# Attention rows scaled on GpSimd, two attention stages ordered by feature tile, value products ahead of turns

## The chip, the cores and the metric

One core of one Trainium2 chip runs the whole kernel in one launch. The metric is the device time in microseconds (us); the time quoted is the median of several runs.

## The reference, cut to what matters

The program is four layers of a transformer on 512 tokens of 1024 features, all in float32. Two of its parts are touched here. Both are attention with 16 query heads and 4 key/value heads of 64 features.

```
# sparse attention (NSA), first layer: two branches, "selected" and "window"
p_s = softmax(where(dist_s >= 0, q k_s + bias_s, NEG));  o_s = p_s v_s
p_w = softmax(where(m_w,         q k_w + bias_w, NEG));  o_w = p_w v_w
o = gate0 * o_c + gate1 * o_s + gate2 * o_w
y = (o * silu(z)) @ w_out
# sliding window attention (SWA), last layer: window of 128 keys and a sink logit per head
p = exp(s - m) / (sum(exp(s - m)) + exp(sink - m));      y = (p v) @ w_o
```

With 512 tokens both NSA branches see every earlier key, so a 128-query tile i (0 to 3) has 128(i+1) keys in NSA, and 256 keys (128 for i = 0) in SWA. The compressed branch o_c is ready before the stage starts and lies in `oT`.

## The kernel before, in words

The kernel is a list of stages (`build`). Every engine runs its part of each stage in order and ends it in `end_stage` (L2894 to L2897), where it waits until TensorE, ScalarE, VectorE and GpSimd have all ended theirs. Large products use three passes: weights and activations are split into a high part (fp32r) and the rest, the low part. ScalarE makes the high part of a weight slot of 512 KB (`split_hi`, L259), GpSimd the low part (`split_lo`, L270); the rings hold three slots.

**NSA, stage `NsaAttend`.** A *pair* is one feature tile k of 128 features (two heads, `st` 0 and 1), one query tile i and one branch br: 64 pairs, in the order i = 3, 2, 1, 0, then k, then br. TensorE works in rounds. Round u issues S(u), T(u-2), V(u-3):
- S, scores (L1264): two products in the two halves of the array, into two of four PSUM banks.
- T, turns (L1275): 2(i+1) transposes of 128x128 of the exponentials, into banks 4 and 5.
- V, value products (L1288): 2(i+1) products into bank 6 + br.

VectorE adds the bias and takes the row minimum (L1368), ScalarE takes the exponential with the row sum (L1325). VectorE copies the turned head 0 out of PSUM (L1377), ScalarE head 1 (L1333). The row sums are divided out only later. After every 8 pairs (a *batch*: four k, two branches) VectorE makes the reciprocals times the gate (L1383, L1386), TensorE spreads these columns over the 64 features of each head with 16 small products (L1298), and VectorE copies the spread out of PSUM and multiplies with banks 6 and 7 (`combine`, L1393 and L1394). The next batch's first V waits for that (L1284), since it writes the same banks. GpSimd then adds the two branches into `oT` and multiplies by z (L1352, L1353, L1355).

**Output, after NSA.** Only when the stage has ended on all engines does ScalarE round `oT` to the high part (L785) and VectorE and GpSimd take the low part (L897, L836), tile k by tile k, and TensorE's projection (L358 high, L368 low, in `project_tokens`) waits for each.

**SWA, stage `SwaAttend`.** The same scheme: 32 pairs (i, k), i outermost, batches of 4. L1955 are its scores, L1966 turns, L1978 value products, L1989 the spread, L2056 the bias, L2021 the exponential, L2065 and L2029 the copies (VectorE two thirds of them, ScalarE every third pair). VectorE and ScalarE also work out the sink's term per batch (L2072, L2042, L2079, L2080), and `combine` is L2087 and L2088. The spread here takes a turn in the four score banks, so the next scores wait for `combine`. `SwaProject` comes before it and also splits the first two weight slots of the output projection; `NsaAttend` splits its two at its own start.

Of the kernel before, what the change touches and what calls it, by code (L numbers as in the profile page):

```python
# [7 lines left out]
ALU = mybir.AluOpType  # L8
# [6 lines left out]
P = 128  # L15
T = 512
# [427 lines left out]
class Stage:  # L444
    def __init__(self, env):
        self.env = env
# [258 lines left out]
class Output(Stage):  # L705
# [3 lines left out]
    def __init__(self, env, w_out, g_row, oT, o=None, z=None, kd=KD, following=None, whole=None):  # L709
        super().__init__(env)  # L710
        self.o, self.oT, self.kd, self.g_row, self.z, self.whole = o, oT, kd, g_row, z, whole
# [5 lines left out]
        if o is not None or whole is not None:  # L717
            env.ots += KD
# [35 lines left out]
    def turned(self, k):  # L754
        if self.whole is not None:
            return self.whole[:, k, :]
# [20 lines left out]
    def scalar(self, act, step):  # L777
        env, nc = self.env, self.env.nc
        env.split_hi(act, self.lds[0])
        for k in range(KD if self.o is not None or self.whole is not None else 0):  # L780
            if self.z is not None:
                act.wait_ge(env.otmp_ready, self.tmp0 + k + 1)
            elif self.o is not None:
# [44 lines left out]
    def gpsimd(self, pool, step):  # L828
# [3 lines left out]
        if self.z is not None or self.whole is not None:  # L832
# [16 lines left out]
    def vector(self, dve, step):  # L849
        env, nc = self.env, self.env.nc  # L850
        if self.whole is not None:
            for k in range(0, KD, 2):
                self.low(dve, k)
# [353 lines left out]
class PairAttend(Attend):  # L1207

    def __init__(self, env, prefix, pairs, per):
# [3 lines left out]
        self.scale_ready, self.spread_ready = env.sem(prefix + "scale_ready"), env.sem(prefix + "scale_spread")  # L1215

        self.uses = []
        for step in range(len(pairs) + 4):
            if step < len(pairs):
                self.uses.append(("scores", step))  # L1220
            if step >= per + 2 and (step - 2) % per == 0:
                self.uses.append(("spread", (step - 2) // per - 1))
        self.use = {key: n for n, key in enumerate(self.uses)}

    def banks(self, kind, n):
        at = 2 * (self.use[kind, n] % 2)
        return self.env.ps[:, at:at + 2, :]

    def wait_banks(self, pe, kind, n):

        at = self.use[kind, n] - 2
        if at >= 0:
            before, m = self.uses[at]
            if before == "scores":
                pe.wait_ge(self.s_biased, 2 * m + 2)
            else:
# [1783 lines left out]
```

## Time and profile before

| | |
|---|---|
| median of 3 runs | 2593.06 us (2592.02 to 2595.28) |
| the profiled execution's own time | 2606.13 us |
| its span, first to last instruction | 2604.3 us |
| TensorE matmuls busy | 2266.0 us (87%) |
| ScalarE, VectorE, GpSimd busy | 983.2, 926.0, 794.2 us |
| mean granted TensorE clock | 0.886 of full speed |

The span is one execution's; 1.8 us lie around it. Busy matmul time is modelled, so what TensorE's idle time and the rounds' lengths say counts for more than its busy share.

### The profile page before, as it was taken

To read this page: it belongs to the slowest core of one execution; us is meant where nothing else is said; L and a number is where in the kernel's file an instruction comes from. 1 tells how busy PE (TensorE), PEld (TensorE's weight loads), DVE (VectorE), ACT (ScalarE), POOL (GpSimd) and SP (SyncE) were. 2 spreads that over 40 slices of the span, in tenths; PEclk is the share of its full clock that TensorE was granted. 3 is DMA by queue.
4 is the path that set the end of the run, shared out by engine and by line. 5 is a ranking of instruction groups with operands and counts; after the bars stand their busy time and mean duration, and the time that the engine had idled before them with its cause. 6 is when DMAs were issued, how large, how long until landed. Compare 5 with 4: busy or idle time off the path is not lost.

```text
span 2604.3 us, 32281 instructions
## 1 busy us (share of the span) xinstructions
PE 2266.0 (87%) x12952; PEld 1782.8 (68%) x12954; DVE 926.0 (36%) x1861; ACT 983.2 (38%) x1841; POOL 794.2 (30%) x376
## 2 busy tenths in 40 slices
PE   5999788799987879984599969999897888999898
PEld 4898565578765647743488647888687656888787
DVE  1100455430028464257343354333104164333401
ACT  3331255442245353353134425444215344444412
POOL 2331011234420324324000143444442303444442
PEclk9987699699998879966569879999999989999999
DMA  4222000023220112201101022333322202333322
GB/s 121 74 69 76 22 1 1 9 81 92 89 73 1 61 49 77 83 4 25 31 7 27 28 81 65 97 93 96 107 94 73 66 1 65 89 97 94 94 96 81
DMA packets 222423, 162.16 MB, mean 62 GB/s; under 512 B 31451, under 2 KB 206115, under 8 KB 222275
## 3 DMA queue, kind: packets, MB, share of 16 engines
q1 hardware_dynamic: 219762, 151.91, 19.9%
q0 software_dynamic: 2512, 8.19, 1.0%
q8 instruction: 104, 1.70, 0.3%
q14 instruction: 45, 0.36, 0.0%
HBM read 154.83 MB, written 5.24 MB: 61 GB/s over the span
## 4 chain that ended last, share of the span: by engine, by line
PE 52%; DVE 8%; ACT 3%; issue 2%; DMA 1%; POOL 1%; POOLq 0%; DVEq 0%; SPq 0%; ACTq 0%; PEld 0%; PEldq 0%
PE ps L358 11%; PE ps L329 8%; PE ps L328 8%; PE ps L332 8%; PE ps L368 5%; PE ps L2581 2%; PE ps L2539 2%; PE ps L1955 1%; PE ps L1966 1%; PE ps L1978 1%; ACT buffer L2636 1%; DVE buffer L2207 1%; PE ps L2604 1%; PE ps L2551 1%; PE ps L2230 1%
## 5 line engine op out<-in xcount | busy, mean ns | idle before, releaser
L270 POOL TENSOR_TENSOR weights_lo<-buffer,weights_hi 128x1024 fp32r<-128x1024 f32 (+1 forms) x265 | 658.3, 2486 | 1017.7 <-ACT weights_hi L259 1017.3
L259 ACT ACTIVATE weights_hi<-buffer 128x1024 fp32r<-128x1024 f32 (+1 forms) x265 | 276.3, 1045 | 315.5 <-PE ps L368 306.6
L328 PE MATMUL ps<-u_hi,weights_hi 128*128 128x512 f32 (+1 forms) x752 | 281.5, 378 | 6.4 <-DVE u_lo L642 5.9
L329 PE MATMUL ps<-u_lo,weights_hi 128*128 128x512 f32 (+1 forms) x752 | 285.1, 383 | 0.0
L332 PE MATMUL ps<-u_hi,weights_lo 128*128 128x512 f32 (+1 forms) x752 | 176.9, 378 | 0.0
L1786 ACT ACTIVATE buffer<-ps,buffer 128x512 f32<-128x512 f32 x88 | 68.5, 779 | 282.6 <-PE ps L332 282.6
L1816 DVE SCALAR_TENSOR_TENSOR buffer<-ps,buffer,buffer 128x511 f32<-128x511 f32 x88 | 66.0, 750 | 292.0 <-ACT buffer L1786 292.0
L328 PEld LDWEIGHTS ps<-u_hi,weights_hi 128*128 128x128 f32 x752 | 143.5, 191 | 33.2 <-DVE u_lo L642 6.5
L2636 ACT ACTIVATE buffer<-ps 32x128 f32<-32x128 f32 (+4 forms) x240 | 92.6, 393 | 188.2 <-PE ps L2581 64.7
L329 PEld LDWEIGHTS ps<-u_lo,weights_hi 128*128 128x128 f32 x752 | 143.1, 190 | 29.3
L332 PEld LDWEIGHTS ps<-u_hi,weights_lo 128*128 128x128 f32 x752 | 136.8, 191 | 26.6 <-POOL weights_lo L270 0.2
L358 PE MATMUL ps<-weights_hi,act_hi 128*128 128x512 f32 x352 | 113.3, 404 | 17.7 <-DVEq L2897 17.7
L872 DVE RECIPROCAL buffer<-buffer 128x1 f32<-128x1 f32 x24 | 3.8, 160 | 347.6 <-ACT buffer L797 347.5
L358 PE MATMUL ps<-weights_hi,act_lo 128*128 128x512 f32 x352 | 112.6, 401 | 0.0
L1325 ACT ACTIVATE buffer<-buffer,buffer 128x512 f32<-128x512 f32 (+3 forms) x128 | 71.5, 558 | 91.2 <-DVE buffer L1368 91.1
L1368 DVE CUSTOM_DVE_ANT_0 buffer<-ps,buffer 128x512 f32<-128x512 f32 (+3 forms) x128 | 62.0, 486 | 88.9 <-PE ps L1264 88.9
L368 PE MATMUL ps<-weights_lo,act_hi 128*128 128x512 f32 x352 | 91.9, 395 | 0.0
L358 PEld LDWEIGHTS ps<-weights_hi,act_hi 128*128 128x128 f32 x352 | 67.8, 193 | 34.2 <-DVEq L2897 18.5
L328 PE MATMUL ps<-nsa_u_hi,weights_hi 128*128 128x512 f32 x192 | 78.7, 410 | 7.4 <-PEq L2897 5.7
L2853 POOL DMA_DIRECT2D buffer<-in_gn_g x1 | 0.6, 600 | 275.1 <-ACTq L2897 275.1
L328 PE MATMUL ps<-mix_hi,weights_hi 128*128 128x512 f32 (+2 forms) x160 | 67.9, 424 | 18.6 <-DVE mix_lo L2195 12.8
L328 PE MATMUL ps<-diff_u_hi,weights_hi 128*128 128x512 f32 (+1 forms) x216 | 78.8, 372 | 4.5 <-DVE diff_u_lo L642 3.4
(380 smaller groups left out, 4625.6 us busy)
## 6 DMA issues: line engine op xcount, KB each, us to landing
buffer<-in_w_up SPq DMA_DIRECT2D x88, 512.0 KB, 3.8
buffer<-in_w_down SPq DMA_DIRECT2D x44, 512.0 KB, 3.2
buffer<-in_diff_w_in SPq DMA_DIRECT2D x32, 512.0 KB, 4.0
buffer<-in_nsa_w_in SPq DMA_DIRECT2D x28, 512.0 KB, 3.8
buffer<-in_w_rkv SPq DMA_DIRECT2D x24, 512.0 KB, 3.8
buffer<-in_nsa_w_out SPq DMA_DIRECT2D x8, 512.0 KB, 3.6
buffer<-in_diff_w_out SPq DMA_DIRECT2D x8, 512.0 KB, 3.5
buffer<-in_norm_g POOLq DMA_DIRECT2D x8, 512.0 KB, 4.0
```

The costliest lines, as they stand in the source:

```text
L259: self.nc.scalar.activation(self.part_hi[:, part % self.PARTS, 0:n], self.raw[:, ld % self.RAW, 0:n], ACT.Copy).then_inc(self.hi_ready, 1)
L270: self.nc.gpsimd.tensor_tensor(self.part_lo[:, part % self.PARTS, 0:n], self.raw[:, ld % self.RAW, 0:n], self.part_hi[:, part % self.PARTS ...
L328: nc.tensor.matmul(out, hi[:, k, :], rhs[0][:, k, tokens], start=(k == 0), stop=False)
L329: nc.tensor.matmul(out, hi[:, k, :], rhs[1][:, k, tokens], start=False, stop=False)
L332: mm = nc.tensor.matmul(out, lo[:, k, :], rhs[0][:, k, tokens], start=False, stop=(k == KD - 1))
L358: nc.tensor.matmul(out(i, b), lhs[part][:, index * m + k, i * P:(i + 1) * P], hi[:, k, b * width:(b + 1) * width], start=(index + k == 0 a ...
L368: mm = nc.tensor.matmul(out(i, b), lhs[0][:, index * m + k, i * P:(i + 1) * P], lo[:, k, b * width:(b + 1) * width], start=False, stop=stop)
L1325: nc.scalar.activation(m.p[:, at, 0:n], m.p[:, at, 0:n], ACT.Exp, scale=-1.0, bias=m.nmax[:, at:at + 1], accum_out=m.psum[:, total:total + ...
L1368: nc.vector.tensor_tensor_reduce(m.p[:, at, 0:n], self.banks("scores", u)[:, st, 0:n], m.bias[:, 2 * k + st, T - n:T], -1.0, 1e38, ALU.add ...
L1786: nc.scalar.activation(m.conv[:, 2 * (j % 2) + half, :], env.bank(g), ACT.Identity, scale=self.col(2, half, j), bias=self.col(3, half, j)) ...
L1816: step(nc.vector.scalar_tensor_tensor(c[:, 1:T], env.bank(g)[:, 0:T - 1], self.col(1, half, j), c[:, 1:T], ALU.mult, ALU.add))
L2636: copy = lambda dst, src: nc.scalar.activation(dst, src, ACT.Copy)
```

## The change

- In both stages k becomes the outer loop. NSA's order is (k, i, br) with i = 3, 1, 2, 0; SWA's is (k, i) with i = 3, 2, 1, 0.
- Right after a pair's exponentials VectorE takes the reciprocals of its two row sums (`invert`), and GpSimd multiplies the exponentials by them in place, 128 rows by 128(i+1) columns per head, two instructions per pair; in NSA the gate is a second factor of the same instruction. The spread, `combine`, and the additions on GpSimd are gone.
- A tile k gathers in one PSUM bank, 6 + k % 2: in NSA both branches and all i, 512 columns. One VectorE addition per k takes it into `oT` (`take`); GpSimd multiplies by z and takes the low part, ScalarE the high part. For the last k VectorE does GpSimd's share.
- In SWA GpSimd writes the sink as one more column of the scores, and the exponential and its sum take it in. ScalarE and VectorE take the high and low part of each k straight from PSUM.
- The round is S(u), V(u-4), T(u-3) in place of S(u), T(u-2), V(u-3); the ring of exponentials has four slots in place of three.
- TensorE doesn't wait for the end of these two stages; the output projection waits for tile k's low part and for the banks. The output projection no longer makes the high and low parts.
- One more weight slot is split ahead in both places.

```diff
 class Output(Stage):
     def tensor(self, pe):
-        ready = (lambda k: self.wait_turned(pe, k)) if turns or self.whole is not None else None
+        ready = (lambda k: self.wait_turned(pe, k)) if turns else None
+        if self.before is not None:
+            self.before.wait_banks_free(pe)
+            ready = lambda k: self.before.wait_result(pe, k)
...
 class PairAttend(Attend):
+    AHEAD = 3
+    SLOTS = 4
+    def invert(self, dve, u):
+        at = self.slot(u, 0)
+        dve.wait_ge(self.p_ready, 2 * u + 2)
+        self.env.nc.vector.reciprocal(self.m.scale[:, at:at + 2], self.m.psum[:, at:at + 2]).then_inc(self.inverse_ready, 1)
...
 class NsaAttend(PairAttend):
-        super().__init__(env, "nsa_", [(i, k, br) for i in reversed(range(NT)) for k in range(KD) for br in range(2)], 8)
+        super().__init__(env, "nsa_", [(k, i, br) for k in range(KD) for i in (3, 1, 2, 0) for br in range(2)], 8)
...
     def tensor(self, pe):
         def scores(u):
-            self.wait_banks(pe, "scores", u)
+            if u >= 2:
+                pe.wait_ge(self.s_biased, 2 * (u - 2) + 2)
...
         def turn(u):
             for st in range(2):
-                pe.wait_ge(self.p_ready, 2 * u + st + 1)
+                pe.wait_ge(self.p_scaled, 2 * u + st + 1)
...
-        for step in range(n_pairs + 4):
+        for step in range(n_pairs + self.AHEAD + 1):
             if step < n_pairs:
                 scores(step)
-            if 2 <= step <= n_pairs + 1:
-                turn(step - 2)
-            if 3 <= step <= n_pairs + 2:
-                values(step - 3)
-            if step >= 10 and (step - 2) % 8 == 0:
-                spread((step - 2) // 8 - 1)
+            if step - self.AHEAD - 1 >= 0:
+                values(step - self.AHEAD - 1)
+            if 0 <= step - self.AHEAD < n_pairs:
+                turn(step - self.AHEAD)
...
     def gpsimd(self, pool, step):
+        def scale(u):
+            k, i, br = self.pairs[u]
+            n = P * (i + 1)
+            pool.wait_ge(self.inverse_ready, u + 1)
+            for st in range(2):
+                at, gate = self.slot(u, st), 3 * (2 * k + st) + 1 + br
+                p = m.p[:, at, 0:n]
+                nc.gpsimd.tensor_scalar(p, p, m.scale[:, at:at + 1], m.gate[:, i, gate:gate + 1], ALU.mult,
+                                        ALU.mult).then_inc(self.p_scaled, 1)
...
+        for u in range(n_pairs):
+            scale(u)
+            if u % self.per == 3 and u > self.per:
+                gated(u // self.per - 1)
+            if u % self.per == 7 and u > self.per:
+                low(u // self.per - 1)
...
     def vector(self, dve, step):
+        def take(k):
+            dve.wait_ge(self.pv_done, self.per * (k + 1))
+            o = m.oT[:, k, :]
+            nc.vector.tensor_tensor(o, env.ps[:, 6 + k % 2, :], o, ALU.add).then_inc(self.o_taken, 1)
...
+        for u in range(n_pairs + self.AHEAD):
             if u < n_pairs:
                 bias(u, 0)
+            if u >= self.AHEAD:
+                copy(u - self.AHEAD)
             if u < n_pairs:
                 bias(u, 1)
+            if 1 <= u <= n_pairs:
+                self.invert(dve, u - 1)
+            if u % self.per == 4 and u > self.per:
+                take(u // self.per - 1)
...
 class SwaProject(Stage):
-        self.env.split_lo(pool, self.q[-1][0] + 2)
+        self.env.split_lo(pool, self.q[-1][0] + 3)
...
 class SwaAttend(PairAttend):
-        super().__init__(env, "swa_", [(i, k) for i in reversed(range(NT)) for k in range(KD)], 4)
+        super().__init__(env, "swa_", [(k, i) for k in range(KD) for i in reversed(range(NT))], NT)
...
+        def high(k):
+            act.wait_ge(self.pv_done, self.per * (k + 1))
+            nc.scalar.activation(m.u[0][:, k, :], env.ps[:, 6 + k % 2, :], ACT.Copy).then_inc(self.hi_ready, 1)
...
+        def sink(u):
+            k, n, at = self.pairs[u][0], self.width(u), self.slot(u, 0)
+            if u >= self.SLOTS:
+                pool.wait_ge(self.pT_ready, u - self.SLOTS + 1)
+            nc.gpsimd.tensor_copy(m.p[:, at:at + 2, n], m.nsinks[:, 2 * k:2 * k + 2]).then_inc(self.sink_put, 1)
+        def scale(u):
+            pool.wait_ge(self.inverse_ready, u + 1)
+            for st in range(2):
+                at = self.slot(u, st)
+                p = m.p[:, at, 0:self.width(u)]
+                nc.gpsimd.tensor_scalar(p, p, m.scale[:, at:at + 1], None, ALU.mult).then_inc(self.p_scaled, 1)
...
+        def low(k):
+            dve.wait_ge(self.hi_ready, k + 1)
+            nc.vector.tensor_tensor(m.u[1][:, k, :], env.ps[:, 6 + k % 2, :], m.u[0][:, k, :].bitcast(F32),
+                                    ALU.subtract).then_inc(self.lo_ready, 1)
...
-def end_stage(env, eng, s):
+def end_stage(env, eng, s, goes_on=False):
     eng.drain().then_inc(env.stage_done, 1)
-    eng.wait_ge(env.stage_done, 4 * (s + 1))
+    if not goes_on:
+        eng.wait_ge(env.stage_done, 4 * (s + 1))
```

## Rows read from the trace of the kernel before

**Rows 1.** Windows (stretch, length, PE, PEld, DVE, ACT, POOL busy, clock, DMA) of both stages.
```profile
314.00:516.80 202.80, 171.59 (x1474) 112.45 (x1473) 108.77 (x353) 101.15 (x324) 34.20 (x28) 0.87 0.02 6
2071.90:2160.40 88.50, 72.94 (x593) 47.70 (x593) 54.18 (x191) 43.26 (x151) 1.00 (x2) 0.83 0.02 7
```

**Rows 2.** Timeline around the first batch border of NSA: start us, us, engine, line.
```profile
346.73 1.09 PE L1275 MATMUL ps<-buffer,buffer 128*128 128x128 f32 x8
...
349.91 1.23 DVE L1394 TENSOR_TENSOR buffer<-ps,buffer 128x1024 f32<-128x1024 f32 x1
...
351.28 1.98 PE L1288 MATMUL ps<-buffer,buffer 128*64 128x128 f32 x16 [3.46 <-DVE buffer L1394]
```

**Rows 3.** Windows of 5 us in NSA; the third number from the end is the clock.
```profile
341.00:346.00 5.00, 5.00 (x62) 3.87 (x63) 2.06 (x6) 2.65 (x7) 0.00 (x0) 1.00 0.01 2
...
351.00:356.00 5.00, 4.72 (x24) 2.92 (x25) 0.83 (x3) 0.00 (x0) 3.80 (x3) 0.50 0.00 0
476.00:481.00 5.00, 5.00 (x28) 2.68 (x24) 1.69 (x12) 2.83 (x14) 1.55 (x2) 0.50 0.02 5
```

**Rows 4.** Timeline, end of NSA and start of its output projection.
```profile
505.04 1.22 PE L1288 MATMUL ps<-buffer,buffer 128*64 128x128 f32 x8
...
516.80 1.19 PE L358 MATMUL ps<-weights_hi,nsa_u_hi 128*128 128x512 f32 x2 [8.36 <-DVE nsa_u_lo L897]
...
518.81 3.93 DVE L897 TENSOR_TENSOR nsa_u_lo<-buffer,nsa_u_hi 128x512 fp32r<-128x512 f32 x2 [0.57 <-ACT nsa_u_hi L785]
```

**Rows 5.** Timeline, the start of weight slots 1 and 3 (counted from 0) of that projection.
```profile
524.20 0.62 PE L358 MATMUL ps<-weights_hi,nsa_u_hi 128*128 128x512 f32 x2
...
535.27 0.62 PE L358 MATMUL ps<-weights_hi,nsa_u_hi 128*128 128x512 f32 x2
```

**Rows 6.** Timeline, TensorE's scores and turns of an i = 2 round, and the next scores.
```profile
388.28 0.92 PE L1264 MATMUL ps<-buffer,buffer 64*128 64x384 f32 x4
389.12 0.87 PE L1275 MATMUL ps<-buffer,buffer 128*128 128x128 f32 x6
...
390.73 0.59 PE L1264 MATMUL ps<-buffer,buffer 64*128 64x384 f32 x2
```

**Rows 7.** Timeline, SWA's last pairs (128 keys) at full clock: scores, turns, value products.
```profile
2152.21 0.50 PE L1955 MATMUL ps<-buffer,buffer 64*128 64x128 f32 x4
...
2152.64 0.44 PE L1966 MATMUL ps<-buffer,buffer 128*128 128x128 f32 x2
...
2153.00 0.44 PE L1978 MATMUL ps<-buffer,buffer 128*64 128x128 f32 x4
```

**Rows 8.** Groups by line and shape in NSA (busy us, mean ns of one).
```profile
L1325 ACT ACTIVATE buffer<-buffer,buffer 128x512 f32<-128x512 f32 x32 | 23.0, 719 | 23.9 <-DVE buffer L1368 23.9
L1368 DVE CUSTOM_DVE_ANT_0 buffer<-ps,buffer 128x512 f32<-128x512 f32 x32 | 21.7, 686 | 28.7 <-PE ps L1264 28.7
L1333 ACT ACTIVATE buffer<-ps 128x512 f32<-128x512 f32 x16 | 9.2, 578 | 0.3 <-PE ps L1275 0.3
```

**Rows 9.** GpSimd's groups by line and shape, whole span.
```profile
L270 POOL TENSOR_TENSOR weights_lo<-buffer,weights_hi 128x1024 fp32r<-128x1024 f32 x261 | 654.0, 2507 | 995.8 <-ACT weights_hi L259 995.4
L2419 POOL TENSOR_TENSOR buffer<-buffer,buffer 128x512 f32<-128x512 f32 x8 | 14.1, 1757 | 5.9 <-ACT buffer L2432 5.9
L1352 POOL TENSOR_TENSOR buffer<-buffer,buffer 128x512 f32<-128x512 f32 x8 | 10.1, 1267 | 166.6 <-DVE buffer L1394 166.6
L836 POOL TENSOR_TENSOR nsa_u_lo<-buffer,nsa_u_hi 128x512 fp32r<-128x512 f32 x4 | 6.0, 1523 | 0.1
L2746 POOL MEMSET buffer<- 128x256 f32 x2 | 0.6, 312 | 1.5 <-DVEq L2897 1.5
```

**Rows 10.** Timeline, SWA: scores and turns of 256 keys, and scores after a batch border.
```profile
2105.31 0.70 PE L1955 MATMUL ps<-buffer,buffer 64*128 64x256 f32 x4
2105.94 0.66 PE L1966 MATMUL ps<-buffer,buffer 128*128 128x128 f32 x4
...
2111.99 0.49 PE L1955 MATMUL ps<-buffer,buffer 64*128 64x256 f32 x2 [2.12 <-DVE buffer L2088]
```

More of the change, by code:

```diff
@@ L779, in scalar @@
         env.split_hi(act, self.lds[0])
-        for k in range(KD if self.o is not None or self.whole is not None else 0):
+        for k in range(KD if self.o is not None else 0):
             if self.z is not None:
                 act.wait_ge(env.otmp_ready, self.tmp0 + k + 1)
-            elif self.o is not None:
+            else:
                 act.wait_ge(env.tr_ready, self.tr0 + k + 1)
@@ L831, in gpsimd @@
         pool.dma_start(env.post_g, self.g_row.partition_broadcast(P)).then_inc(env.g_arrived, 16)
-        if self.z is not None or self.whole is not None:
+        if self.z is not None:
             env.split_lo(pool, self.lds[0])
@@ L1214, in __init__ @@
         self.act_copied = env.sem(prefix + "probsT_act_copied")
[L1215 to L1236, printed above, removed]
-                pe.wait_ge(self.o_taken, m + 1)
+        self.inverse_ready = env.sem(prefix + "inverse_ready")
+        self.p_scaled = env.sem(prefix + "probs_scaled")
@@ L1994, in tensor @@
-        for step in range(n_pairs + 4):
+        for step in range(n_pairs + self.AHEAD + 1):
             if step < n_pairs:
                 scores(step)
-            if 2 <= step <= n_pairs + 1:
-                turn(step - 2)
-            if 3 <= step <= n_pairs + 2:
-                values(step - 3)
-            if step >= 6 and (step - 2) % 4 == 0:
-                spread((step - 2) // 4 - 1)
+            if step - self.AHEAD - 1 >= 0:
+                values(step - self.AHEAD - 1)
+            if 0 <= step - self.AHEAD < n_pairs:
+                turn(step - self.AHEAD)
@@ L2082, in combine @@
-        def combine(b):
-            i, k = self.pairs[4 * b]
-            dve.wait_ge(self.pv_done, 4 * b + 4)
-            dve.wait_ge(self.spread_ready, b + 1)
-            o = m.oT[:, k:k + 4, i * P:(i + 1) * P]
-            step(nc.vector.tensor_copy(o, self.banks("spread", b)[:, 0, :].rearrange("p (k t) -> p k t", t=P)))
-            nc.vector.tensor_tensor(o, env.ps[:, 6 + b % 2, :].rearrange("p (k t) -> p k t", t=P), o,
-                                    ALU.mult).then_inc(self.o_taken, 1)
@@ L2091, in vector, with low @@
-        for u in range(n_pairs + 4):
+        def low(k):
+            dve.wait_ge(self.hi_ready, k + 1)
+            nc.vector.tensor_tensor(m.u[1][:, k, :], env.ps[:, 6 + k % 2, :], m.u[0][:, k, :].bitcast(F32),
+                                    ALU.subtract).then_inc(self.lo_ready, 1)
+        for u in range(n_pairs + self.AHEAD):
             if u < n_pairs:
                 bias(u, 0)
-            if 2 <= u <= n_pairs + 1 and self.copier[u - 2] == "D":
-                copy(u - 2)
+            if u >= self.AHEAD and self.copier[u - self.AHEAD] == "D":
+                copy(u - self.AHEAD)
@@ L2096, in vector @@
             if u < n_pairs:
                 bias(u, 1)
-            if u >= 3 and (u + 1) % 4 == 0 and u < n_pairs:
-                shift((u + 1) // 4 - 1)
-            if u >= 5 and (u - 1) % 4 == 0:
-                scale((u - 1) // 4 - 1)
-            if u >= 7 and (u - 3) % 4 == 0:
-                combine((u - 3) // 4 - 1)
+            if 1 <= u <= n_pairs:
+                self.invert(dve, u - 1)
+            if u % self.per == 1 and u > 2 * self.per:
+                low(u // self.per - 2)
@@ L2106 @@
+        low(KD - 1)
 class RwkvMemory:
@@ L2917, in build @@
             NsaCompressed(env, m),
-            NsaAttend(env, m, len(env.loads) + 1),
-            Output(env, io["nsa_w_out"][0], post[0], m.u, whole=m.oT, following=(pre[1], dm.u)),
+        ]
+        nsa = NsaAttend(env, m, len(env.loads) + 2)
+        stages += [
+            nsa,
+            Output(env, io["nsa_w_out"][0], post[0], [m.o_hi, m.o_lo], following=(pre[1], dm.u), before=nsa),
             DiffProject(env, dm),
```

283 lines of the change are left out of this document (131 added, 152 removed).

## The prediction, made before the changed kernel was run

> **What bounds the kernel now.** I read the page first: TensorE is 87% busy and every other engine under 40%, so only what keeps TensorE waiting or slow can pay. The windows over the two stages show 202.5 us for NSA from its first scores to the first projection matmul, and 88.5 us for SWA, at a mean granted clock of 0.87 and 0.83 [rows 1]. There are only two clock levels, 2.4 and 1.2 GHz, so about 26% and 34% of these stretches ran at the lower one.
>
> Then the timeline at a batch border [rows 2]: turns end at 347.8, the spread is in PSUM, VectorE multiplies until 351.1, and the next value products start at 351.28 after 3.46 us of idle TensorE. With eight batches there are seven such borders in NSA. The windows behind them [rows 3] show the second price: full clock before the wait, 1.2 GHz after it; and in the last query tiles, where rounds are short, the clock is 1.2 GHz for whole windows. SWA has the same wait in front of the scores, 2.12 us [rows 10]. At the end of NSA the last value products are issued at 505, the projection starts at 516.80 [rows 4]: spread, combine, three GpSimd passes, the barrier, the first high and low parts, all in series.
>
> **TensorE's work that stays.** An i = 2 round at full clock is S 0.84, T 0.81, and 2.45 in all [rows 6]; with one key tile S is 0.43, T 0.37, so 1.17 in all [rows 7]; with two, S 0.63 and T, V 0.59, 1.81 [rows 10]. A key tile thus adds 0.64, and i = 3 takes 3.1. A feature tile k has each i twice: 2 x (3.1 + 2.45 + 1.81 + 1.17) = 17.1 us, eight of them 137 us against 202.5. A k of SWA is 3 x 1.81 + 1.17 = 6.6, eight of them 53 us against 88.5. What is left to ask is whether the others keep up.
>
> **GpSimd's price.** No row has its multiply by a column. From below: a fill that reads nothing, 0.31 us for 256 columns, so 0.62 for 512. From above: its two-input multiply or add of the same shape, 1.27 [rows 9]. The new one reads one stream of the two, so it lies between; I take the middle, 0.95 for 512 columns, in proportion for fewer. Per k in NSA that is 4 x 0.95 x 2.5 = 9.5 us, at the upper end 12.7, and 2.8 more for the z product (1.27) and the low part (1.52). So 12.3 to 15.5 us per 17.1: not the bound. VectorE has 108.8/8 = 13.6 us per eighth now [rows 1]; combine's two passes of 1.2 each [rows 2] and the small ones go (-2.9), eight reciprocals (some 0.16 each, an estimate) and one 0.69 addition come: 12.7. ScalarE has 101.2/8 = 12.6, plus 0.6 for the high part.
>
> *Contention.* The low parts of the projection show it: VectorE took 3.93 us for two subtractions with GpSimd working beside it [rows 4], where a 512-column pass takes it 0.69 [rows 8], and GpSimd's own took 1.52 in place of 1.27 [rows 9]. In that pair both of VectorE's inputs lie in SBUF. In the attention rounds one lies in PSUM, and GpSimd's passes there stayed at 1.27. I take no contention. The Trainium skill, GPSIMD Engine Reference, Specifications, states the same line: GpSimd contends with VectorE instructions that have two SBUF inputs or run in a two-port mode. By it the sum stays; by the contended 1.76 us that another stage shows (L2419, [rows 9]) GpSimd would need 20.4 us per k, which is a rival below.
>
> **A period of eight NSA rounds, engine by engine.** A round is S(u), V(u-4), T(u-3). V waits for the copies of the turns that ended the round before, so only S covers them: ScalarE's copy needs 0.58 plus some 0.1 of latency for 512 columns. The order 3, 1, 2, 0 puts S of i = 2 over the copy of i = 3 (0.84 over 0.7), 3 over 2, 1 over 0, and 0 over 1 (0.43 over 0.48: 0.05 to 0.1 late, twice). Where two i = 3 pairs are followed by short rounds (1.4 us), ScalarE still has two exponentials of 0.72 to do and its copy comes about 0.2 late. The reciprocal of pair u comes after the bias of pair u+1, GpSimd then has from early in round u+2 to the end of round u+3, some 2.5 us at the tightest place against 1.9 (middle) or 2.54 (upper) for an i = 3 pair; at the upper end one turn per period is 0.5 late, 4 us in all. The period is 17.1 + 0.4 = 17.5. With no wait over 0.3 us in it I take the clock as full.
>
> NSA then: fill 6.7 us until round 4 (one pair waits for the new latency, and GpSimd first splits a third slot, 2.5 us [rows 9], of which 1 us shows); 60 rounds, 131 us; drain 5 us, without S as cover; the last addition 0.75, for which the projection's banks wait. Sum 143.5 against 202.5: **-59**. GpSimd's z product and the low part of the last tile now lie beside the projection. Its first weight slot took 524.20 - 516.80 = 7.4 us at low clock and behind the low parts; later ones take 11.07/2 = 5.5 [rows 4, 5]: **-1.9**.
>
> **SWA.** GpSimd's third split stands before the stage's barrier, behind the second, and TensorE waits for it: **+2.4**. The copies here are of 512 columns, 0.69 on VectorE, under S of 0.63: each such V is late by some 0.15 (ScalarE's third of them 0.05), and the low part, 0.69 on VectorE once per k, makes a copy some 0.3 late. VectorE has 54.2/32 = 1.7 us per pair now [rows 1]; without combine's copy and the sink's sums, with reciprocals, 1.55, near TensorE's 1.65. GpSimd needs 2 x 0.48 + 0.15 = 1.1 per full pair (upper 1.4). So 7.4 per k, seven k to go after a fill of 6.3: 52; drain 5.7; high and low part of the last k in series, 1.45, since they hold the last bank. Sum with the split 67.9 against 88.5: **-20.6**; the projection's first slot **-1.5**, not more, since the clock may drop in this last wait.
>
> The ScalarE and VectorE work per batch that goes (sink exponentials, sums) lay beside TensorE: nothing. The sum is -83. The walk ignores semaphore latency in 96 rounds; at 0.07 us each I give back 7, so **-76**: 2606.1 becomes 2530, and against the median of 2593.06, which is 13 below the profiled execution, 2517.
>
> **Rivals.**
> - *GpSimd becomes the bound by contention.* At 1.76 us per 512 columns NSA's period is 20.4, the stage 177 and not 143.5; SWA's 1.9 per full pair stays about under its rounds. Then -76 + 33 = -43: 2550. For: one stage shows 1.76. Against: the passes in this very stage took 1.27.
> - *The clock stays low.* If the stages keep their mean clock (0.87, 0.83), 137/0.87 and 53/0.83 add 20 and 11 us: -45, 2548. For: the short rounds ran at 1.2 GHz for whole windows [rows 3], and SWA keeps small waits each round. Against: short rounds are now spread among long ones, and the windows with full rounds had full clock.
> - *Slower: GpSimd's multiply by a column is far slower than its two-input one.* With a factor f on 1.27, both stages bound by GpSimd take 8(12.7f + 2.8) + 14 and 8(4.5f + 0.6) + 16.4 us. They reach the old 294 (with the first slots) at f = 1.7, 2.2 us per 512 columns; at f = 2 the time is 2593 + 38 = 2631. For: GpSimd has been given 192 passes on the path of every pair, and no row shows the operation. Against: it reads less than the operation at 1.27. The Trainium skill, GPSIMD Engine Reference, section 4.1, advises against plain elementwise work on this engine, about 2x slower with two inputs, though it puts one input at roughly line rate; no row here shows the latter.
> - *It comes out even*: two of the first three together in mild form.
>
> **Numbers.** Forecast 0.68, contention 0.10, clock 0.14, slower 0.05, even 0.03. The low end takes the sum without the 7 and with GpSimd and the copies hiding fully, -91: 2502. The high end reaches over the two middle rivals: 2552. A measurement of this kernel tells about 0.2%, 5 us, from no change. Faster 0.93, same 0.02, slower 0.05.
>
> **What would show it.** In the changed profile: no PE idle of over 1 us behind VectorE in either stage; scores of the same position in two successive k 17.5 us apart in NSA, 7.4 in SWA; GpSimd's 512-column multiply between 0.62 and 1.27 us; VectorE's bias still 0.69; clock 1.00 in nearly all windows; the first projection matmul of NSA near 458, SWA's 68 us after its old first scores. I am wrong if turns wait for GpSimd in most rounds (contention or price), if the clock in the stages is under 0.95, or if the value products wait for copies by more than 0.3 us per round.

## The result, and the profile after the change

The changed kernel took 2528.40 us against 2593.27 us for the kernel before on the same chip: 0.9749 of its time, with a 95% interval of 0.973 to 0.9768, or 64.9 us less. One of its four executions was disturbed (3090.1 us) and is left out; 2528.40 is the median of the other three (with it the median is 2529.87). The forecast was 76 us less, so the direction and the range held and the gain was overstated by 11 us.

The first lines of the page of the changed kernel:

```profile
span 2526.6 us, 31732 instructions
...
PE 2211.2 (88%) x12568; PEld 1737.9 (69%) x12570; DVE 888.1 (35%) x1895; ACT 985.2 (39%) x1833; POOL 904.9 (36%) x582
```

GpSimd is busy for 111 us more than before, VectorE for 38 less. The whole is shorter all the same, so the busy time of GpSimd did not bound it. The profiled spans differ by 77.7 us, 13 more than the medians. That execution of the kernel before was itself 13 us over its median, and 12 us of the difference lie in stages that the change does not touch. By stretches, the two profiles say this:

| stretch | before | after | forecast |
|---|---|---|---|
| NSA, first scores to first projection matmul | 202.5 | 152.4 | 143.5 |
| the same to the last high-part matmul of the projection | 248.8 | 196.9 | |
| SWA, first scores to first projection matmul | 88.5 | 72.4 | 65.5 |
| the same to the last high-part matmul | 135.5 | 119.6 | |
| wait ahead of SWA's first scores | 4.2 | 6.5 | +2.4 |

NSA with its projection gives 51.8 us and SWA 15.9 less 2.3, together 65.4; the medians say 64.9.

Windows of the changed kernel: the two stages, then 10 us of NSA's fill, 10 us well behind it, and 5 us of SWA's fill. The columns are those of [rows 1].

```profile
314.60:467.00 152.40, 141.89 (x1217) 89.81 (x1216) 96.09 (x393) 108.16 (x327) 98.56 (x145) 0.98 0.04 12
2009.68:2082.12 72.44, 59.66 (x465) 35.62 (x465) 45.41 (x190) 43.46 (x147) 57.05 (x96) 0.90 0.03 9
316.00:326.00 10.00, 7.84 (x42) 4.66 (x39) 5.35 (x22) 6.20 (x19) 7.45 (x8) 0.68 0.51 156
346.00:356.00 10.00, 9.68 (x93) 6.32 (x92) 6.57 (x27) 7.21 (x23) 6.68 (x11) 1.00 0.01 2
2015.00:2020.00 5.00, 4.50 (x20) 2.52 (x20) 1.95 (x9) 2.56 (x10) 4.97 (x8) 0.50 0.00 0
```

Against [rows 1] NSA's clock went from 0.87 to 0.98, SWA's from 0.83 to 0.90. The windows of 1.2 GHz inside NSA [rows 3] are gone; what is left of them in the stages lies in the two fills and in SWA's last microsecond. The stretch that held the first batch border [rows 2] is a full-clock window like the others.

What TensorE and GpSimd wait for, in NSA (us in total, times, longest us; PEld is the weight load, which runs ahead of its product):

```profile
POOL buffer L1353 <- DVE buffer L1233: 48.5, 42, 4.4
PEld ps L1291 <- DVE buffer L1393: 35.0, 63, 0.9
PE ps L1291 <- ACT buffer L1320: 6.1, 18, 0.7
PE ps L1278 <- POOL buffer L1353: 1.0, 1, 1.0
```

GpSimd (L1353) waits for the reciprocals and is ahead of its work. TensorE's products wait for it once, in the fill. In its place V (L1291) waits for the copies of the turns: its weight load in 63 of 64 rounds, and by the records 18 times the product itself. Not each of these waits costs time. One round that loses, in the timeline, from the V before it:

```profile
391.20 0.88 PE L1291 MATMUL ps<-buffer,buffer 128*64 128x128 f32 x12
392.00 0.44 PE L1278 MATMUL ps<-buffer,buffer 128*128 128x128 f32 x2
392.37 0.70 PE L1267 MATMUL ps<-buffer,buffer 64*128 64x256 f32 x4
...
393.06 0.25 ACT L1320 ACTIVATE buffer<-ps 128x128 f32<-128x128 f32 x1
...
393.46 0.44 PE L1291 MATMUL ps<-buffer,buffer 128*64 128x128 f32 x4 [0.39 <-ACT buffer L1320]
...
394.20 0.70 PE L1267 MATMUL ps<-buffer,buffer 64*128 64x256 f32 x4
```

T (L1278) is issued at 392.00. VectorE copies as soon as it ends, but ScalarE has a high part and an exponential to do first and copies only at 393.06 (L1320). S (L1267) is issued at 392.37 and is 0.63 us of work, and V starts 1.09 behind it, 0.46 late: the round takes 1.83 us, and TensorE's own work in it is 1.38. In another round that loses, ScalarE copies 0.09 us after the turns' end and has no queue to speak of; there the cover is too short:

```profile
401.66 0.49 PE L1267 MATMUL ps<-buffer,buffer 64*128 64x128 f32 x4
...
401.82 0.36 ACT L1320 ACTIVATE buffer<-ps 128x256 f32<-128x256 f32 x1
...
402.33 0.66 PE L1291 MATMUL ps<-buffer,buffer 128*64 128x128 f32 x8 [0.18 <-ACT buffer L1320]
```

S of i = 0 is 0.43 us of work, and V starts 0.67 behind it. Of the eight rounds of a period four lose nothing (V starts 0.84 and 1.06 behind S of i = 2 and i = 3, which is S's own work). The two behind copies of i = 1 lose 0.24 and 0.21, the two behind copies of i = 0 lose 0.46 and 0.08, together 0.99. So the scores of the same position in two successive k stand 18.06 us apart (17.5 in the forecast), TensorE's own work being 17.07:

```profile
369.40 1.13 PE L1267 MATMUL ps<-buffer,buffer 64*128 64x512 f32 x4
...
387.47 1.13 PE L1267 MATMUL ps<-buffer,buffer 64*128 64x512 f32 x4
```

The timeline at the end of NSA, which answers to [rows 4] and to slot 1 of [rows 5]:

```profile
465.78 0.44 PE L1291 MATMUL ps<-buffer,buffer 128*64 128x128 f32 x4 [0.46 <-ACT buffer L1320]
466.26 0.69 DVE L1399 TENSOR_TENSOR buffer<-ps,buffer 128x512 f32<-128x512 f32 x1 [0.72 <-PE ps L1291]
...
467.00 0.74 PE L358 MATMUL ps<-weights_hi,nsa_u_hi 128*128 128x512 f32 x2 [0.78 <-DVE buffer L1399]
...
472.66 0.62 PE L358 MATMUL ps<-weights_hi,nsa_u_hi 128*128 128x512 f32 x2
```

The projection follows the last V by 1.2 us, one addition, in place of 11.8, and its first slot takes 5.66 us in place of 7.4.

Groups by line and shape of the changed kernel: GpSimd's and VectorE's bias in NSA, then GpSimd's in SWA (L2070); they answer to [rows 8, 9]:

```profile
L1353 POOL TENSOR_SCALAR buffer<-buffer,buffer,buffer 128x512 f32<-128x512 f32 x32 | 24.1, 765 | 1.3 <-DVE buffer L1233 1.3
L1384 DVE CUSTOM_DVE_ANT_0 buffer<-ps,buffer 128x512 f32<-128x512 f32 x32 | 21.7, 686 | 14.2 <-PE ps L1267 13.2
L1353 POOL TENSOR_SCALAR buffer<-buffer,buffer,buffer 128x256 f32<-128x256 f32 x32 | 17.4, 555 | 21.1 <-DVE buffer L1233 21.1
L1359 POOL TENSOR_TENSOR buffer<-buffer,buffer 128x512 f32<-128x512 f32 x7 | 8.9, 1274 | 0.0
...
L2070 POOL TENSOR_SCALAR buffer<-buffer,buffer 128x256 f32<-128x256 f32 x48 | 43.7, 922 | 9.0 <-DVE buffer L1233 9.0
L2070 POOL TENSOR_SCALAR buffer<-buffer,buffer 128x128 f32<-128x128 f32 x16 | 9.5, 603 | 1.5 <-DVE buffer L1233 1.5
```

NSA's multiply lies between the bounds of the forecast (0.62 to 1.27 for 512 columns), and the bias kept its 686 ns: no contention shows. SWA's multiply does not lie between them: 922 ns for 256 columns, where NSA's instruction with one factor more takes 555. In proportion to 512 columns it is 1.84 us, outside the upper bound.

SWA's k takes 7.92 us (six k in 47.52), 7.4 in the forecast, TensorE's own work 6.6. In the timeline these are its second and last scores of 128 keys (first fence), and a stretch between them in which V (L2002) waits for ScalarE's copy, which stands behind a high part and an exponential (second fence):

```profile
2024.83 0.49 PE L1980 MATMUL ps<-buffer,buffer 64*128 64x128 f32 x4
...
2072.35 0.49 PE L1980 MATMUL ps<-buffer,buffer 64*128 64x128 f32 x4
```

```profile
2045.73 0.66 PE L1990 MATMUL ps<-buffer,buffer 128*128 128x128 f32 x4
...
2046.03 0.57 ACT L2042 ACTIVATE swa_u_hi<-ps 128x512 fp32r<-128x512 f32 x1
...
2046.32 0.70 PE L1980 MATMUL ps<-buffer,buffer 64*128 64x256 f32 x4
...
2047.00 0.58 ACT L2038 ACTIVATE buffer<-ps 128x512 f32<-128x512 f32 x1
...
2047.63 0.66 PE L2002 MATMUL ps<-buffer,buffer 128*64 128x128 f32 x8 [0.61 <-ACT buffer L2038]
```

Two readings were open. The value products stand ahead of the turns and wait for copies that only the scores cover; or SWA is bound by its dear multiply, since GpSimd needs 7.5 us per k there (six times 0.922, two times 0.603, four sink columns of 0.19; the records overlap a little). And there was the question how much of the whole belongs to which part of the change.

### The profile page after: what moved, and what is told of

It is laid out like the page before. It is cut to its first block, busy times and chain, and to the rows that moved or that the text cites. A ratio compares the mean times of both kernels' runs of the same rounds, so it can differ in the third digit from the quotient of the medians.

```text
span 2526.6 us, 31732 instructions
## 1 busy us (share of the span) xinstructions
PE 2211.2 (88%) x12568; PEld 1737.9 (69%) x12570; DVE 888.1 (35%) x1895; ACT 985.2 (39%) x1833; POOL 904.9 (36%) x582
## 4 chain that ended last, share of the span: by engine, by line
PE 52%; DVE 8%; ACT 4%; issue 2%; DMA 1%; POOL 1%; POOLq 0%; DVEq 0%; ACTq 0%; SPq 0%; PEld 0%; PEldq 0%
PE ps L358 11%; PE ps L329 8%; PE ps L328 8%; PE ps L332 8%; PE ps L368 5%; PE ps L2594 2%; PE ps L2552 2%; ACT buffer L2649 1%; DVE buffer L2220 1%; PE ps L2617 1%; PE ps L2002 1%; PE ps L2243 1%; PE ps L1990 1%; POOL weights_lo L270 1%; DVE mix_lo L2208 0%
## 5 line engine op out<-in xcount | busy, mean ns | idle before, releaser
L328 PEld LDWEIGHTS ps<-u_hi,weights_hi 128*128 128x128 f32 x752 | 143.5, 191 | 33.9 <-DVE u_lo L644 7.3
L1353 POOL TENSOR_SCALAR buffer<-buffer,buffer,buffer 128x512 f32<-128x512 f32 (+3 forms) x128 | 76.4, 607 | 49.1 <-DVE buffer L1233 48.5
```

What stands on the lines that cost most here:

```text
L328: nc.tensor.matmul(out, hi[:, k, :], rhs[0][:, k, tokens], start=(k == 0), stop=False)
L1353: nc.gpsimd.tensor_scalar(p, p, m.scale[:, at:at + 1], m.gate[:, i, gate:gate + 1], ALU.mult, ALU.mult).then_inc(self.p_scaled, 1)
```

## The experiments

Every ratio is against the kernel before in runs on the same chip; the changed kernel ran on one chip, e1 to e4 on a second, e5 to e8 on a third, e9 and e10 on a fourth. "Stage" is the stretch from first scores to first projection matmul.

| run | edit to the changed kernel | median us | ratio (95%) | NSA | SWA |
|---|---|---|---|---|---|
| (changed) | | 2528.40 | 0.9749 (0.973 to 0.9768) | 152.4 | 72.4 |
| e1 | SWA as before | 2539.4 | 0.9791 (0.9775 to 0.9808) | 152.4 | 88.1 |
| e2 | SWA's multiply with a second factor 1.0 | 2530.11 | 0.9759 (0.9738 to 0.9779) | 152.4 | 70.6 |
| e3 | turns first, then value products | 2510.39 | 0.9683 (0.9664 to 0.9703) | 142.6 | 65.8 |
| e4 | two weight slots split ahead | 2520.47 | 0.9725 (0.9706 to 0.9743) | 150.4 | 72.3 |
| e5 | i = 3, 2, 1, 0 in NSA | 2530.59 | 0.9746 (0.9731 to 0.976) | 153.1 | 72.2 |
| e6 | TensorE waits at the stage ends | 2530.07 | 0.9746 (0.973 to 0.9762) | 154.5 | 71.1 |
| e7 | one more GpSimd pass per head in NSA | 2551.07 | 0.9827 (0.9808 to 0.9847) | 173.8 | 72.4 |
| e8 | e2, e3 and e4 together | 2498.77 | 0.9623 (0.9609 to 0.9637) | 140.6 | 59.7 |
| e9 | e8 with two rounds ahead, not three | 2551.85 | 0.9823 (0.9795 to 0.9852) | 175.0 | 80.4 |
| e10 | e8, NSA's multiply with one factor | 2528.05 | 0.9738 (0.9699 to 0.9778) | 166.2 | 59.7 |

### e1: the NSA part alone

SWA with its order, spread, `combine` and output as in the kernel before, NSA changed.

```diff
-class SwaAttend(PairAttend):
+class OldPair(Attend):
...
-        self.env.split_lo(pool, self.q[-1][0] + 3)
+        self.env.split_lo(pool, self.q[-1][0] + 2)
```

> The changed kernel with its SWA part (stage, memory, projection after it, third weight slot) as in the kernel before; only NSA is changed. Theory: the gain is the sum of two local gains, 51.5 us up to the stage after NSA and 13.6 us in SWA and its projection, as the starts of the stages stand in the two traces; so this kernel should take 2593 - 51 = 2542 us. Rival: part of the gain comes from elsewhere (the clock in the stages between, where the two profiled executions also differ by some 12 us); then this kernel keeps more than 51, up to 63 us, and comes under 2533.

The NSA part alone gives 52.4 us by the medians and the SWA part the rest, 11 by the ratios and 13.6 by the profiles. NSA is 152.4 as with both, and SWA is back at 88.1 us with a clock of 0.83. The two parts add; the miss is in both of them.

### e2: a second factor in SWA's multiply

```diff
-                nc.gpsimd.tensor_scalar(p, p, m.scale[:, at:at + 1], None, ALU.mult).then_inc(self.p_scaled, 1)
+                nc.gpsimd.tensor_scalar(p, p, m.scale[:, at:at + 1], 1.0, ALU.mult, ALU.mult).then_inc(self.p_scaled, 1)
```

> GpSimd's multiply in SWA gets a second factor of 1.0, so that it is the same form as NSA's (two operations in place of one and none); the values are unchanged. Theory: GpSimd bounds SWA in the changed kernel because its one-operation form takes 922 ns for 256 columns, where NSA's two-operation form takes 555; with the second factor it takes 555, a feature tile of SWA falls from 7.9 to about 7.3 us, and the kernel is some 5 us faster than the changed one. Rival: the form is not the cause (another buffer stride, other neighbours); then the instruction stays at 0.92 us and nothing moves.

The group of the multiply in its SWA:

```profile
L2070 POOL TENSOR_SCALAR buffer<-buffer,buffer 128x256 f32<-128x256 f32 x48 | 22.3, 477 | 17.4 <-DVE buffer L1233 17.4
```

The multiply takes half the time, 477 ns, and GpSimd's busy time in the stage falls from 57.1 to 33.1 us, but the narrow scores still stand 7.92 us apart (2033.43 to 2080.95 for six k). The 1.8 us that the stage is shorter lie in the fill. Its first four rounds take 6.2 us in place of 7.1, since the first turns wait less for the multiply (1.2 us in place of 1.9). The rest came with the clock, which rose earlier (0.93 over the stage, 0.90 before); in e6, whose SWA fill has the same instructions as the changed kernel's, it rose earlier too, and the stage took 71.1. Against the changed kernel the whole time did not move by more than the intervals, where 5 us less had been expected. SWA's GpSimd was not the bound, though its work per k was within 0.5 us of the k.

### e3: turns ahead of value products

Both stages, the rounds S(u), T(u-3), V(u-4), all else as changed.

```diff
             if step < n_pairs:
                 scores(step)
-            if step - self.AHEAD - 1 >= 0:
-                values(step - self.AHEAD - 1)
             if 0 <= step - self.AHEAD < n_pairs:
                 turn(step - self.AHEAD)
+            if step - self.AHEAD - 1 >= 0:
+                values(step - self.AHEAD - 1)
```

> Undoes one part in both stages: the round is S(u), T(u-3), V(u-4) again, turns ahead of value products, everything else as changed. Theory: in the changed kernel V waits for the copies of the turns just before it, covered by S alone; with T between them no V waits for a copy, and GpSimd has slack in NSA, so NSA's period of eight rounds falls from 18.06 towards the 17.1 of TensorE's own work (7 us in all); in SWA, where GpSimd is near its limit, little. Rival, the reason that the order could have been chosen for: the turns then come earlier by one V, before GpSimd has scaled, and wait for it; then the period stays or grows, with PE idle before L1278 behind POOL.

This is 18 us faster than the changed kernel (2510.39 against 2528.40; 17 by the ratios), where 7 and a little had been expected. NSA is 9.8 us shorter and SWA 6.6. SWA's projection took another 2.5 us less in this profile, at a clock of 1.00 in place of 0.94, but that is not the work of the edit: in e5, which leaves SWA alone, it did the same. NSA's period is 17.07 us: TensorE's own work and nothing else. SWA's k is 7.29 us (2013.77 to 2057.54 for six k), and there the turns now wait for the multiply. The waits of its SWA:

```profile
DVE buffer L2098 <- PE ps L1990: 8.6, 16, 2.0
PEld ps L1990 <- POOL buffer L2070: 8.6, 16, 1.9
```

The order that the forecast took as given was the largest single cost in the changed kernel. GpSimd's work for SWA was a bound hidden under it, as e8 shows.

### e4: two slots split ahead, as before

```diff
-        self.env.split_lo(pool, self.q[-1][0] + 3)
+        self.env.split_lo(pool, self.q[-1][0] + 2)
...
-        env.split_hi(act, self.q[-1][0] + 3)
+        env.split_hi(act, self.q[-1][0] + 2)
...
-        nsa = NsaAttend(env, m, len(env.loads) + 2)
+        nsa = NsaAttend(env, m, len(env.loads) + 1)
```

> Only two weight slots are split ahead, as in the kernel before, in front of SWA and in NSA. Theory: the third split stands before SWA's barrier and delays its first scores by 2.4 us, and in NSA it holds GpSimd until 319.4, so that the first turns wait 1 us and TensorE falls to the low clock; without it SWA's first scores come 2.4 us sooner and NSA's fill is 1 to 3 us shorter; 3 to 5 us in all. Rival: the projection then waits for its third slot and gives it back; then the start of the fourth slot of each projection stays where it is.

NSA's stage is 2.0 us shorter, all of it in the fill, and the wait ahead of SWA's first scores is 2.3 shorter. That is 4.3 us of the 8 between the medians; by the ratios the difference is 6, and its intervals overlap slightly. SWA's stage did not move, and its projection was 2.5 shorter at a clock of 1.00, as in e5, which does not touch it. The third slot brought nothing that the profile shows: the projections are no slower with two.

### e5 and e6: the order of i, and the stage ends

```diff
-        super().__init__(env, "nsa_", [(k, i, br) for k in range(KD) for i in (3, 1, 2, 0) for br in range(2)], 8)
+        super().__init__(env, "nsa_", [(k, i, br) for k in range(KD) for i in (3, 2, 1, 0) for br in range(2)], 8)
```

> The changed kernel with NSA's query tiles in the order 3, 2, 1, 0 in place of 3, 1, 2, 0; round order as changed (value products first). Theory: V(u-4) waits for copies that only S(u) covers, so the order decides which scores lie over which copy; with 3, 2, 1, 0 the scores of i = 1 (0.63 us) lie over the copies of i = 3 (0.7) and those of i = 0 (0.43) over i = 2 (0.57); the period grows from 18.06 to some 18.5 to 19 us, 4 to 8 us in all. Rival: what makes V late is ScalarE's queue (exponentials of i = 3 in front of the copies in short rounds), whatever lies over the copy; then this order, in which long rounds follow long ones, is as fast or faster.

The period is 18.53 us and not 18.06; over eight k and with a clock of 1.00 against 0.98 the stage is 0.7 us longer. NSA's projection took 47.1 us in place of 44.6 and SWA's 44.6 in place of 47.1, at clocks that had changed places, 0.94 and 1.00. The whole time is the same within the intervals, where 4 to 8 us more had been expected. The order 3, 1, 2, 0 is worth about half a microsecond per k while V waits for copies; no run has the other order with turns first.

```diff
-        self.tensor_goes_on = True
+        self.tensor_goes_on = False
```

> TensorE waits for the end of both attention stages again, as all other engines do; everything else as changed. Theory: in NSA the last tile's z product, high and low part (467.0 to 469.1 in the changed profile) then stand in front of the projection, +2.3 us; in SWA TensorE already waits for the last low part, so nothing: 2 to 3 us in all, and perhaps 1 to 2 more where the wait drops the clock. Rival: the barrier was worth more, since it also held the weight splits and the queues of the next stage; then 5 us or more.

With the barriers NSA's stage is 2.1 us longer, and its projection 1.5 more, at a clock of 0.96 in place of 1.00. That 1.5 cannot be laid to the barrier, since in e5, which has none, the projection lost 2.5 in the same way. SWA shows no loss. The whole is unchanged within the intervals. What removed the serial end of [rows 4] was that high and low parts are made per k inside the stage, hardly that TensorE skips the barrier.

### e7: a second GpSimd pass per head

The same exponentials multiplied by 1.0 once more, NSA only.

```diff
+                nc.gpsimd.tensor_scalar(p, p, 1.0, 1.0, ALU.mult, ALU.mult).then_inc(self.once, 1)
+                pool.wait_ge(self.once, 2 * u + st + 1)
                 nc.gpsimd.tensor_scalar(p, p, m.scale[:, at:at + 1], m.gate[:, i, gate:gate + 1], ALU.mult,
                                         ALU.mult).then_inc(self.p_scaled, 1)
```

> In NSA GpSimd multiplies each tile of exponentials by 1.0 before the real multiply, so its work per tile doubles; the values are unchanged. Theory: GpSimd is not NSA's bound in the changed kernel (9.7 us of multiplies in a period of 18.06) and becomes it at double price: 2 x 9.7 + 2.5 and some 1 to 2 us of waits, 22 to 24 us per period, so NSA takes 32 to 48 us more. Rival: GpSimd has hidden slack beyond that, or its latency already sets the period; then it grows by less than 2 or by the full 9.7 (78 us in all).

The groups of the added pass, for 512 and 128 columns:

```profile
L1354 POOL TENSOR_SCALAR buffer<-buffer 128x512 f32<-128x512 f32 x32 | 19.9, 620 | 0.5 <-DVE buffer L1233 0.5
...
L1354 POOL TENSOR_SCALAR buffer<-buffer 128x128 f32<-128x128 f32 x32 | 9.6, 300 | 1.6 <-DVE buffer L1233 1.6
```

GpSimd's work per k goes from 12.3 us (four times 0.765, 0.662, 0.555 and 0.448, and 2.54 for z and the low part) to 19.6, and the period from 18.06 to 20.9 (388.11 to 409.01). The stage is 21.4 us longer, the whole 23 by the medians and 20 by the ratios, where 32 to 48 had been expected. The step came out smaller because the pass by constants is cheaper than the one by columns, and because GpSimd had time to spare. It shows where GpSimd becomes the bound: some 5 us of its time per k were to spare, 7.3 were asked for, and the period ended 1.3 over the work. The forecast's formula for a bound GpSimd, eight times its work plus 14 us, gives 171 for 173.8 measured.

### e8: turns first, two slots, second factor

The edits of e2, e3 and e4 together, as quoted above.

> Turns first, SWA's multiply with a second factor of 1.0, and two weight slots split ahead, together. Theory: with turns first nothing waits for copies, so now GpSimd's 922 ns form does bound SWA (its feature tile took 7.3 us against 6.6 of TensorE's work) and the two-operation form, 477 ns, brings it to about 6.8: 4 us; the two slots save 2.4 us in SWA and some in NSA; 2510 becomes 2502 to 2505 us, faster than the kernels before and after. Rival: SWA is then bound by VectorE (copies, biases and reciprocals, some 6.4 us per feature tile with waits) and stays near 7.2: 2507.

This is the fastest version of the study: 2498.77 us, 96.5 less than the kernel before and 30 less than the changed one (33 by the ratios). NSA's period is 17.07 us and SWA's k is 6.59 (2015.18 to 2048.15 for five k), TensorE's own 17.1 and 6.6 of the forecast's first step. One k of its SWA has no wait in it:

```profile
2028.38 0.49 PE L1980 MATMUL ps<-buffer,buffer 64*128 64x128 f32 x4
2028.80 0.66 PE L1990 MATMUL ps<-buffer,buffer 128*128 128x128 f32 x4
2029.38 0.44 PE L2002 MATMUL ps<-buffer,buffer 128*64 128x128 f32 x4
2029.75 0.70 PE L1980 MATMUL ps<-buffer,buffer 64*128 64x256 f32 x4
...
2034.95 0.49 PE L1980 MATMUL ps<-buffer,buffer 64*128 64x128 f32 x4
```

With e2 and e3 it makes a table of two by two for the time of one SWA k, and that settles the two readings. (e8 also has two slots in place of three; in e4 that alone left SWA's k at 7.92.)

| | one factor, 922 ns | second factor, 477 ns |
|---|---|---|
| value products first | 7.92 | 7.92 (e2) |
| turns first | 7.29 (e3) | 6.59 (e8) |

With value products first GpSimd's price makes no difference; with turns first it makes all of it. Each cause hid the other.

### e9: two rounds ahead

e8 with the turns two rounds behind the scores, as in the kernel before.

```diff
-    AHEAD = 3
+    AHEAD = 2
```

> The fastest kernel so far (turns first, second factor in SWA, two slots) with turns two rounds after the scores in place of three, as in the kernel before; four slots of exponentials stay. Theory: the third round is what GpSimd's pass needs; the reciprocal of pair u is taken after the bias of pair u+1, so with turns in round u+2 each turn waits for GpSimd: PE idle before L1278 behind POOL in most rounds, NSA's period 20 to 25 us in place of 17.07 and SWA's feature tile 8 to 10 in place of 6.6; 2499 becomes 2540 to 2575. Rival: VectorE and ScalarE run far enough ahead of TensorE for two rounds to do, and the fill is a round shorter; then it is within 5 us of 2499.

Its waits in NSA, by the product and by the weight load of the turns:

```profile
PE ps L1278 <- POOL buffer L1353: 15.4, 21, 1.5
...
PEld ps L1278 <- POOL buffer L1353: 57.0, 100, 1.9
```

It is 53 us slower than e8 (52 by the ratios); NSA's period is 21.2 us (376.48 to 397.67) and SWA's k about 9. The multiply adds a step between exponential and turn, and without a third round TensorE waits for it in most rounds, above all with the weight load. Of the two shifts in the change, that of the turns from u-2 to u-3 is needed, and the swap of T and V is not.

### e10: one factor in NSA's multiply

e8 with the gates of the two branches left out, so that NSA's multiply has one factor.

```diff
-                nc.gpsimd.tensor_scalar(p, p, m.scale[:, at:at + 1], m.gate[:, i, gate:gate + 1], ALU.mult,
-                                        ALU.mult).then_inc(self.p_scaled, 1)
+                nc.gpsimd.tensor_scalar(p, p, m.scale[:, at:at + 1], None, ALU.mult).then_inc(self.p_scaled, 1)
```

> The same fastest kernel, with NSA's multiply in the one-operation form: the gate is left out of the two branches, so the program computes less than it should there. Theory: the one-operation form is the slow one for any width (922 ns for 256 columns and 600 for 128 give 2.5 ns per column, so 1.56 us for 512, where the two-operation form takes 0.77); GpSimd then has 17.3 + 2.5 = 19.8 us of work per period and bounds NSA: period 19.8 to 20.5 in place of 17.07, 22 to 28 us more. Rival: the 922 ns belong to SWA's buffers or neighbours; then the 256-column multiply stays at 0.55 here and the time stays at 2499.

The groups of its multiply in NSA:

```profile
L1353 POOL TENSOR_SCALAR buffer<-buffer,buffer 128x512 f32<-128x512 f32 x32 | 49.5, 1561 | 2.8 <-DVE buffer L1233 2.8
...
L1353 POOL TENSOR_SCALAR buffer<-buffer,buffer 128x256 f32<-128x256 f32 x32 | 29.0, 921 | 0.3 <-DVE buffer L1233 0.3
```

The instruction with less to compute takes twice as long: 1561 against 765 ns. NSA becomes bound by GpSimd (period 20.2 us against 17.07), and the kernel loses 29 us to e8. It is the price of the form and not of the stage: 921 ns for 256 columns here, 922 in SWA.

## Why the forecast was right, and where it was wrong

**Right: what bound the kernel.** The seven borders with their wait and the low clock behind them, and the serial end, were the price. They are gone, and the two stages with NSA's projection account for 65.4 us. TensorE's own work per k, 17.1 and 6.6 us, was right to 0.03 us: e8 runs at both (17.07 and 6.59), e3 at the first.

**Right: GpSimd in NSA, no contention, full clock.** 12.3 us of work per k was the forecast's middle case and the measured one. The sum came out so close by luck: for 512 columns the multiply took 0.765 us and not 0.95, for 128 it took 0.448 and not 0.24, and the errors cancel. The contended 1.76 us did not appear; the z product took 1.274 and the bias 686 ns. That agrees with the line that the Trainium skill, GPSIMD Engine Reference, Specifications, draws at VectorE instructions with two SBUF inputs: VectorE's biases, copies and additions in NSA's rounds read at most one input from SBUF. The clock rival fell with the clock of 0.98 in NSA; in SWA, at 0.90, a small part of it came true, in the fill. Two of the forecast's own signs of being wrong appeared in SWA: a clock under 0.95, and value products late by more than 0.3 us per round (1.33 us in the four rounds of a k). In NSA neither did.

**Wrong: the cover of the value products.** The step that failed is "V waits for the copies of the turns that ended the round before, so only S covers them", the step with 0.4 us per period for NSA and 0.5 to 0.8 per k for SWA. The mechanism stood there; its size was too small. The period measured 18.06, 1.0 over TensorE's work, and SWA's k 7.92, 1.3 over. Two terms were short in NSA. Under the scores of i = 0 the walk had V 0.05 to 0.1 late, twice, and it is 0.24 and 0.21: ScalarE's copy and what lies around it take 0.67 from the issue of S where the walk had 0.48. And where ScalarE's copy queues, the walk had 0.2 for two exponentials; with the high part, which it did not place in the order, it is 0.46 and 0.08. In SWA a V behind VectorE's copy is 0.22 late (0.15 in the walk), and twice in three k a V behind ScalarE's queue is 0.69 and 0.98 late, which the walk did not have. e3 removes the swap alone and gets 17.07 us. The forecast priced the swap without asking what the round would be without it, and so did not see that a part of the change was a loss.

**Mis-sized: NSA's ends.** The first four rounds took 7.5 us (6.7 in the sum) and the fifth 4.9, at 1.2 GHz, about 2 more than at full clock. In the drain V has no scores ahead of it and waits 0.67, 0.67, 0.46 and 0.46 for its copies, so that the drain took 6.4 us for the 5 of the sum. With 0.56 per period over 7.5 periods, 4.2, the sum is 143.5 + 0.8 + 2 + 4.2 + 1.4 = 151.9; measured were 152.4.

**Mis-sized: SWA.** 7.92 in place of 7.4 is 3.6 us over seven k, and the other 3.2 lie mostly in the fill and the two rounds behind it, at 1.2 GHz up to about 2023: the first four rounds take 7.1 us for 6.3, and those at 2016.81 and 2020.06 take 3.25 and 3.06 us, where later ones of their kind take about 2. The split ahead of the barrier was right: 2.3 for 2.4.

**The first slots.** NSA's came as forecast, 5.66 for 7.4. SWA's did not: its stage ends in a wait of 1.4 us behind the low part, and the projection starts at 1.2 GHz after it as before, so the 1.5 did not come. In e3, e4 and e5 the same wait of 1.4 us was followed by full clock, and the projection took 44.6 us in place of 47.1; no run tells what decides it.

**The 7 us given back** as a reserve for latencies (0.07 us a round, worked out from no row) covered less than half of the 17.6 by which the sum of -83 was off.

**The slower rival** was nearer than its chance of 0.05 says. In SWA the multiply is 1.45 times the two-input price (922 ns against half of 1.27 us), and the rival decided from 1.7 in both stages. Its formula gives 8(4.5 x 1.45 + 0.6) + 16.4 = 73 us at this factor for a measured 72.4 + 2.3 = 74.7. The agreement is by luck: e2 halves the price and the k does not move. Had NSA's form been the dear one as well, the changed kernel would have had 19.8 us of GpSimd work per k; e10, with a better order, loses 29 us by it.

**Open.** The forecast gave the order of i no price of its own; e5 puts it near 0.5 us per k, within the uncertainty of the whole. Why one factor costs twice as much as two on GpSimd no run here tells, nor whether other operations share it.

## What to carry to other kernels

When a change reorders what one engine issues, walk the order without that part too: value products ahead of turns left the copies with one product's cover in place of two, and cost 17 to 18 us where the whole change brought 65. A stage can be held by two causes of nearly the same size, and then taking away either shows less than it is worth, or nothing; try them together before one is called harmless. And when a new instruction decides the bound, time its exact form in a small experiment first; its neighbours in the profile did not give its price.

## What was not expected of the hardware

On GpSimd a multiply by a column of 128 values cost, for 512, 384, 256 and 128 columns of float32: with two column factors 765, 662, 555 and 448 ns; with the constants 1.0 and 1.0 (e7) 620, 514, 407 and 300 ns; with one column factor and no second operation (e10) 1561, 1242, 921 and 602 ns. With one column factor and the constant 1.0 (e2) it was 477 and 372 ns for 256 and 128. A second operation thus cuts the time to about half for 256 columns and more, and to 0.6 to 0.75 of it for 128. The forms with two operations grow by some 0.83 ns per column over a fixed 200 to 340 ns, the one with a single operation by 2.5 ns over about 280. All of them ran beside VectorE at work, and in every run NSA's bias took 686 or 687 ns for 512 columns.
